# A staged operand loaded in four separate steps and later, one of its sums later, and the first output piece summed by parts

## The reference

```python
h = rms_norm(z, norm_w[l])
q, fz, iv, g_hg, u, g_pool, m_hg, m_pool = split(h @ w_in[l] + b_in[l])   # 8 parts of width 1024
o = rms_norm(hgrn2(q, k, iv, log_f), hg_norm_w)                           # linear recurrence
y_hg = (o * silu(g_hg)) @ w_down_hg[l]                                    # first down projection
y_pool = (mixed * pool_scale * silu(g_pool)) @ w_down_pool[l]             # second down projection
merged = sigmoid(m_hg) * y_hg + sigmoid(m_pool) * y_pool
z = z + merged @ w_out[l]
return rms_norm(z, final_norm_w)[:, N_META:]
```

## Time and profile before

| | |
|---|---|
| time, median of 3 runs | 1051.72 us (1051.66 to 1052.27) |
| profiled execution: its own time | 1051.71 us |
| profiled execution: its span | 1050.0 us |
| PE busy | 1026.1 us, 98% of the span |
| DVE busy | 780.1 us, 74% |
| ACT busy | 491.7 us, 47% |
| DMA | 105.65 MB, mean 101 GB/s |

### The profile page before, as it was taken

One profiled execution on the slowest core, in us unless ns is written; L12 is line 12 of the kernel. 1 busy time (PEld: TensorE's weight loads), 2 busy tenths in 40 slices (PEclk: granted clock), 3 DMA queues, 4 the chain that ended last, 5 costly groups with the idle time before them and its releaser, 6 DMA issues.

```text
span 1050.0 us, 18490 instructions
## 1 busy us (share of the span) xinstructions
PE 1026.1 (98%) x7252; PEld 836.4 (80%) x7252; DVE 780.1 (74%) x1276; ACT 491.7 (47%) x834; POOL 97.3 (9%) x166
## 2 busy tenths in 40 slices
PE   7999999999999999999999999999999999999997
PEld 7777888888888888878888887788887787787886
DVE  7979787878786969696676876864479789979234
ACT  7664636363636363644353433434457346336222
POOL 6200000000010101020101001011100110000111
PEclk9999999999999999999999999999999999999999
DMA  7221111111020202121312122137323774555233
GB/s 275 51 81 62 42 61 42 62 39 64 29 75 22 80 22 82 41 92 41 101 45 98 54 86 91 61 121 270 130 81 101 257 264 160 172 189 174 78 102 130
DMA packets 36630, 105.65 MB, mean 101 GB/s; under 512 B 4640, under 2 KB 4640, under 8 KB 36544
## 3 DMA queue, kind: packets, MB, share of 16 engines
q1 hardware_dynamic: 22352, 66.14, 19.6%
q0 software_dynamic: 8528, 27.31, 7.2%
q10 hardware_dynamic: 5664, 11.02, 2.9%
HBM read 79.28 MB, written 25.17 MB: 99 GB/s over the span
## 4 chain that ended last, share of the span: by engine, by line
PE 81%; DVE 13%; issue 3%; ACT 1%; POOL 1%; DMA 0%; DVEq 0%; ACTq 0%
PE acc L1254 69%; PE levels L1396 2%; DVE w_lo L1637 2%; PE miscs L1418 1%; PE miscs L1430 1%; PE miscs L1429 1%; PE acc L1300 1%; DVE r_lo L2190 1%; PE miscs L1254 1%; PE levels L1254 1%; DVE att L1791 1%; DVE qx L1810 1%; PE miscs L1409 1%; PE miscs L1436 1%; DVE kt L1807 1%
## 5 line engine op out<-in xcount | busy, mean ns | idle before, releaser
L1254 PE MATMUL acc<-r_hi,w_hi 128*128 128x512 f32 x1112 | 445.8, 401 | 8.9 <-DVE r_lo L2190 4.4
L1254 PE MATMUL acc<-r_hi,w_lo 128*128 128x512 f32 x1112 | 434.2, 390 | 0.0
L1254 PE MATMUL acc<-r_lo,w_hi 128*128 128x512 f32 x1112 | 433.6, 390 | 0.0
L1254 PEld LDWEIGHTS acc<-r_hi,w_hi 128*128 128x128 f32 x1112 | 208.8, 188 | 64.5 <-issue 17.2
L1254 PEld LDWEIGHTS acc<-r_hi,w_lo 128*128 128x128 f32 x1112 | 208.7, 188 | 45.1
L1254 PEld LDWEIGHTS acc<-r_lo,w_hi 128*128 128x128 f32 x1112 | 209.1, 188 | 39.9
L749 ACT ACTIVATE w_hi<-sum 128x512 fp32r<-128x512 f32 x156 | 97.8, 628 | 162.7 <-DVE sum L1671 81.9
L1637 DVE TENSOR_TENSOR w_lo<-sum,w_hi 128x512 fp32r<-128x512 f32 x156 | 106.5, 686 | 60.2 <-ACT w_hi L749 59.8
L1637 DVE TENSOR_TENSOR w_lo<-raws,w_hi 128x512 fp32r<-128x512 f32 x120 | 82.1, 687 | 58.9 <-ACT w_hi L749 58.8
L749 ACT ACTIVATE w_hi<-raws 128x512 fp32r<-128x512 f32 x120 | 74.5, 623 | 26.9 <-PE acc L1254 26.9
L1254 PE MATMUL acc<-wo_hi,m_hi 128*128 128x512 f32 x128 | 49.9, 390 | 0.6 <-DVE wo_lo L2326 0.6
(11 more groups left out here) (295 smaller groups left out, 1362.5 us busy)
## 6 DMA issues: line engine op xcount, KB each, us to landing
raws<-in_wstream SPq DMA_DIRECT2D x88, 512.0 KB, 3.6
xin<-in_x SPq DMA_DIRECT2D x8, 512.0 KB, 6.2
a_spill<-gt POOLq DMA_DIRECT2D x16, 256.0 KB, 3.4
c_spill<-pg POOLq DMA_DIRECT2D x16, 256.0 KB, 2.7
stage<-a_spill ACTq DMA_DIRECT2D x4, 1024.0 KB, 13.8
smh_spill<-zq POOLq DMA_DIRECT2D x16, 256.0 KB, 2.4
gate_in<-smh_spill SPq DMA_DIRECT2D x16, 256.0 KB, 5.3
part_spill<-zq POOLq DMA_DIRECT2D x16, 256.0 KB, 5.2
```

The source lines that it names most:

```text
L1254: ins = pe.matmul(out_ap, a, b, start=first and n == 0, stop=final and n == 2, skip_group_check=partial)
```

## The change

1. `load_stage(f, n)` issues one load where it issued two. The first projection's four loads are issued at one place as before. Those of the second are issued one by one: b11 behind product 4 of pair 33, b12 behind product 6, b22 and b21 behind products 2 and 3 of pair 34. Before, two stood behind product 2 and two behind product 5 of pair 33.
2. DVE makes the second `v5` behind product 4 of pair 34, where it stood behind product 1.
3. The first output piece (v = 0) has a function of its own, `first_output`: all eight hi by hi matmuls, then the eight with `wo_lo`, then the eight with `m_lo`. Before, the three stood together for each k, and the first wait of each k was for its `wo_lo` and its `m_lo`.

```diff
@@ ACT
             def load_stage(f, n):
                 src = (a_dram, c_dram)[f]
-                for dst, half, t in ((b11, 0, 0), (b12, 0, 1), (b22, 1, 1), (b21, 1, 0))[2 * n:2 * n + 2]:
-                    act.dma_start(dst[:, :, :], src[4 * half:4 * half + 4, t].rearrange("k p t -> p k t")) \
-                        .then_inc(stage_loaded[n], 16)
+                dst, half, t = ((b11, 0, 0), (b12, 0, 1), (b22, 1, 1), (b21, 1, 0))[n]
+                act.dma_start(dst[:, :, :], src[4 * half:4 * half + 4, t].rearrange("k p t -> p k t")) \
+                    .then_inc(stage_loaded[n // 2], 16)
...
-                        load_stage(0, 0)
-                        load_stage(0, 1)
+                        for n in range(4):
+                            load_stage(0, n)
...
-                    elif p == P_DH + 1 and i == 2:
+                    elif p == P_DH + 1 and i == 4:
                         act.wait_ge(S["r_lo"], 7)
                         load_stage(1, 0)
-                    elif p == P_DH + 1 and i == 5:
+                    elif p == P_DH + 1 and i == 6:
                         load_stage(1, 1)
+                    elif p == P_DH + 2 and i in (2, 3):
+                        load_stage(1, i)
@@ PE
+            def first_output(s):
+                t = T_ORDER[0] // 4
+                for k in (0, 1, 2, 3, 4, 5, 7, 6):
+                    pe.wait_ge(S["wo_hi"], k // 2 + 1)
+                    pe.wait_ge(S["m_hi"], M_SPLIT_AT[k, t])
+                    pe.matmul(out_bank(0)[:, :], m_hi[k][:, s], wo_hi[0][:, k, :], start=k == 0, stop=False,
+                              skip_group_check=True)
+                for k in (0, 1, 2, 3, 4, 5, 7, 6):
+                    pe.wait_ge(S["wo_lo"], k // 2 + 1)
+                    pe.matmul(out_bank(0)[:, :], m_hi[k][:, s], wo_lo[0][:, k, :], start=False, stop=False,
+                              skip_group_check=True)
+                for k in (0, 1, 2, 3, 4, 5, 7, 6):
+                    pe.wait_ge(S["m_lo"], M_SPLIT_AT[k, t])
+                    ins = pe.matmul(out_bank(0)[:, :], m_lo[k][:, s], wo_hi[0][:, k, :], start=False, stop=k == 6,
+                                    skip_group_check=True)
+                ins.then_inc(S["out_mm"], 1)
...
                 s = slice(t * P, (t + 1) * P)
+                if v == 0:
+                    first_output(s)
+                    continue
@@ DVE, pair P_DH + 2
-                elif i == 1:
-                    stage_sum(1, R_V5)
                 elif i == 2:
                     use(P_DH + 2, 0)
+                elif i == 4:
+                    stage_sum(1, R_V5)
```

## The result

| | before | changed |
|---|---|---|
| median of 20 runs | 1052.01 us | 1053.26 us |
| lowest to highest | 1051.26 to 1052.48 | 1052.28 to 1056.48 |
| ratio (95% interval) | | 1.0016 (1.001 to 1.0022) |
| profiled execution: time / span | 1051.71 / 1050.0 us | 1052.78 / 1051.0 us |

The change costs 1.25 us in the median, 0.12%, where +1.16 us was forecast. (The ratio in the table is not the quotient of the two medians, which is 1.0012.) The spread was not forecast: 7 of the changed kernel's 20 runs lie above 1054 us and none of those of before. The runs of before lie within 1.2 us of each other, those of the changed kernel within 4.2.

The account below looks back on a forecast made before the run. TensorE (PE), busy for 98% of the span, was taken as the bound, with DVE the bound from 872.07 to 895.24. 0.25 for v5 plus 0.91 for the first output piece gave +1.16, 1052.9 us; range 1051.4 to 1054.2.

Parts of the forecast that it names:

- The first output piece: Piece 0 on PE: ten matmuls instead of six left behind the wait for wo_lo's last quarter, +0.91 us.
- v5: DVE in pair 34: the sum now stands behind the wait for ACT's w_hi, so PE pays +0.25 us.
- nothing to win there: From 814.67 to 872.07 PE is busy for 57.38 of 57.40 us, so nothing to gain.
- the wrong consumer: PE's product 2 of pair 36, released by DVE's r_lo, was named as meeting DVE's lateness.
- The rival of the full v5 price: Pair 34's gate as late as before, so the whole v5 sum comes on top: +3.0, 1054.7 us; chance 0.10.
- lands earlier: Pair 34's gate load, at 849.71 before, comes earlier because fewer stage loads take DMA bandwidth at its issue.
- b21: Stage load late for V7, landing at 862.9 instead of the expected 855.4: 1057.8 us; chance 0.03.
- The weight loads: Piece 0 pays 8 more exposed weight loads, 1.5 us more: 1054.4 us; chance 0.02.
- Faster: Earlier gates carry DVE ahead into pair 35, part or all of 3.94 us comes back: 1048.7 us; chance 0.05.

Follow-up runs that it names:

- the stage part alone: Kernel before with only the later stage loads and the later v5 sum, first output piece as before: 1052.69 us, ratio 1.0005.
- the slowest execution: Profiled run of the kernel before with only the first output piece summed by parts, stage as before: 1059.25 us, where that kernel's median is 1053.20.
- The profile at 1055.9 us: The changed kernel run once more without any edit, for a second profile: 1055.9 us, one run.

## Why the prediction was right, and where it was not

**The first output piece: right, in mechanism and size.** +0.91 was reckoned from four more matmuls behind an unmoved quarter of `wo_lo`; 0.89 was measured, and the two orders in which only two matmuls, the last ones, need that quarter did not wait for it at all and gained 0.25 (with the two short waits left) and 0.95 (with none).

**v5: the mechanism was right, the term incomplete.** DVE does run late behind `w_hi` and v5. Where the gate was early, in the stage part alone, that is 0.27 us for a forecast of 0.25. In the changed kernel the gate set the time by 0.09 and it is 0.35; the times of 851.85 for 851.87 and 881.83 for 881.9 agree so well by luck, because 0.09 us for the gate and 0.15 lost ahead of 814.8 stand against the 0.29 gained. This gain is what the sum lacked. I took busy time for proof that PE had "nothing to win there" before 872, and 0.29 us were lost at product 6 of pair 33, where the gate came late; the later loads remove that. So in the profiled execution 0.35 and -0.29 all but cancel: +0.05 where +0.25 stood. I also named the wrong consumer. PE meets the lateness at product 6 of pair 35 (0.35 us around 872.34), which waits for DVE's subtraction, and not first at product 2 of pair 36. That does not change the price, since the wait there is as long as before (1.03 us for 1.04). The sum of 1.16 was near the median partly by luck: 0.94 of it is seen in the profiled execution, and the median holds a part of the spread besides.

**The rival of the full v5 price was the other half of the truth.** I gave it 0.10 and reckoned that it sets in once the gate lands after 848.8. The two profiled executions of the changed kernel lie on either side of that: 847.8 and 0.35 us lost; 849.9 and a pause of 1.97 us. What failed was the claim that the gate "lands earlier" and with that the case is closed. In the faster execution it was earlier by 1.9 us only, just past the point where it starts to count, and in the slower one not at all. A chance for it should have been a share of the runs: 7 of 20 are above 1054 us. And its price was short of the halved clock, 1.5 us in the profiled case.

**b21** landed at 855.1 (9.9 us after 845.2) for a V7 at 857.98, reckoned 855.4. **The weight loads** cost nothing, as the first output piece with its last two parts exchanged shows. **Faster**: the later loads do relieve the gates, but DVE's head start ends at `w_hi` and `r_hi`, as argued; what they win is the pause at pair 33 and the spread.

**What stays open** is why the same gate load takes 8 us in one execution and 11 or 13 in the next. That it shares the engines with stage loads and raw weights is what all of these have in common. But the DMA share does not tell them apart: it is 1.04 from 833 to 838.2 in the slowest execution and 1.05 from 833 to 838 in the kernel before, whose gate took 8.0 us. No run took these apart. It is open too whether all seven runs above 1054 us come from the gate. The profile at 1055.9 us shows it in pair 34, and the spread shrinks when v5 alone is put back (2.1 to 0.5 us, 11 runs each); the stage part alone did not reach 4 us in its 11 runs.

## What to carry to other kernels

- Where PE waits for a late operand, count the matmuls behind that wait: four more behind cost 0.9 us. An order in which enough other matmuls stood ahead for the operand to be there gained 0.9. Grouping by kind of operand is worth nothing in itself; the order has to follow the times at which the operands come.
- When work is moved behind a wait for a DMA, look at the slack of that DMA and at what it takes on a bad day. A gate with no slack turned into 0 to 4 us from run to run. The same work ahead of that wait, in DVE's idle time, left a spread of 0.5 us in 11 runs, where 33 of the 35 runs of the kernel before lay within 1.2 us and two above it (1053.26 and 1058.18).
- Read an almost full engine by the starts of its instructions. Busy time hid pauses of 0.3 us here, and these showed where PE first meets a late DVE.

## What the runs showed of the hardware

A pause of PE can cost more than its own length. After 4.43 us of idleness the next 12 matmuls ran at a granted clock of 0.50 (0.43 us apart for 0.227). After 1.81 us of idleness PE ran at the old spacing for 1.3 us more and then at 0.43, with a granted clock of 0.59 over 856 to 860: the clock fell while PE was at work again. After 1.18 us, in the kernel with v5 late and early loads, it stayed at 1.00. The four pauses at the change of operands, two of 1.0 and two of 0.4 us within 14 us in every execution, never did that. A load of 256 KB at the same place took 8.0 us in one execution and 12.8 in another, with the same code for the stage.
